# Slots' tables moved, a held weight piece loaded in the out-projection, router sums copied by two engines, the sample's last columns in one store

## The reference

```python
# u, bg, q, k, v, gates = _project(x, w_in, ...)   one input projection, two head groups
# conv_out = short gated convolution;  attn_out = attention with compressed, selected and window branches
def _post(x, conv_out, attn_out, p, w_out_l, norm_ffn_l, moe_w, norm_ple_l, w_ple_l, w_pg_l, b_pg_l):
    h = x + jnp.concatenate([conv_out, attn_out], axis=-1) @ w_out_l          # out-projection
    hn = rms_norm(h, norm_ffn_l)
    h = h + moe_ffn(hn.reshape(-1, D_MODEL), *moe_w).reshape(h.shape)         # experts
    gate = jax.nn.sigmoid((rms_norm(h, norm_ple_l) @ w_pg_l).astype(jnp.float32) + b_pg_l.astype(jnp.float32))
    return h + (gate * (p @ w_ple_l).astype(jnp.float32)).astype(h.dtype)     # gated embedding

def moe_ffn(h, w_rg, b_rg, w_re, b_re, w_g, w_u, w_d):      # cut: what is computed, not how it is blocked
    p_grp = jax.nn.softmax((h @ w_rg) + b_rg, axis=-1)      # 4 groups
    grp = jnp.argmax(p_grp, axis=-1)                        # the first of them
    le_g = the 8 logits of (h @ w_re) + b_re that belong to grp
    w2, e_loc = lax.top_k(jax.nn.softmax(le_g, axis=-1), 2) # two experts of 32
    w2 = w2 / jnp.sum(w2) * p_grp[grp]
    # for each chosen expert e:  y += w2 * ((silu(h @ w_g[e]) * (h @ w_u[e])) @ w_d[e])
```

## Time and profile before

| | |
|---|---|
| time, median of 3 runs | 905.92 us (903.79 to 905.94) |
| the profiled execution's own time | 907.63 us |
| its span in the trace | 905.7 us |
| PE busy | 888.5 us (98%) |
| DVE busy | 656.8 us (73%) |
| ACT busy | 204.3 us (23%) |
| POOL busy | 70.1 us (8%) |
| moved by DMA | 262.83 MB, mean 290 GB/s |

### The profile page before, as it was taken

The page is one execution under the profiler, slowest core; times in us unless marked ns, Lnnn a source line. Parts: engine busy times, 40 slices in busy tenths (PEclk is TensorE's granted clock), DMA queues, the critical chain, the costliest instruction groups (busy, mean ns, idle before and its releaser), DMA issues.

```text
span 905.7 us, 11854 instructions
## 1 busy us (share of the span) xinstructions
PE 888.5 (98%) x4539; PEld 464.1 (51%) x4539; DVE 656.8 (73%) x1290; ACT 204.3 (23%) x475; POOL 70.1 (8%) x72
## 2 busy tenths in 40 slices
PE   8999999999999999999999999999999999999998
PEld 7866998776544446444333433334434333333544
DVE  6568986668767764565867768678687686757895
ACT  4122231018645204411111111111111111111411
POOL 4021061000000000110000000000000000000000
PEclk9999999999999999999999999999999999999999
DMA  9752835530008776899999999999999999999502
GB/s 302 221 200 71 248 98 173 185 123 1 1 1 194 287 268 228 314 380 422 416 428 426 425 424 427 425 424 425 427 420 423 420 422 421 420 423 379 215 24 76
DMA packets 70269, 262.83 MB, mean 290 GB/s; under 512 B 11882, under 2 KB 38006, under 8 KB 53412
## 3 DMA queue, kind: packets, MB, share of 16 engines
q1 hardware_dynamic: 64864, 250.73, 70.9%
q0 software_dynamic: 4080, 8.93, 2.9%
q10 hardware_dynamic: 1268, 2.40, 0.7%
HBM read 254.95 MB, written 13.08 MB: 296 GB/s over the span
## 4 chain that ended last, share of the span: by engine, by line
PE 82%; DMA 9%; DVE 4%; SPq 3%; ACT 1%; issue 1%; POOLq 0%; DVEq 0%; ACTq 0%
PE ps L1451 75%; DMA w<-in_w_exp_down 4%; DMA w<-in_w_exp_up 4%; SPq L522 3%; PE ps L1946 2%; PE ps L2233 1%; PE ps L1475 1%; DMA h<-in_x_prompt 1%; PE ps L2274 1%; DMA xg<-hn_rows,sidx 1%; PE ps L1486 0%; PE ps L1949 0%; PE ps L1749 0%; PE ps L1639 0%; DVE probs L3098 0%
## 5 line engine op out<-in xcount | busy, mean ns | idle before, releaser
L1451 PE MATMUL ps<-w,xe 128*64 128x512 f32 x1024 | 228.1, 596 | 3.6 <-DMA w<-in_w_exp_up 3.5
L3516 DVE TENSOR_TENSOR h<-h,ps 128x1024 f32<-128x1024 f32 x120 | 143.2, 1215 | 104.6 <-PE ps L1451 104.5
L1451 PEld LDWEIGHTS ps<-w,xe 128*64 128x64 f32 x1024 | 70.1, 137 | 142.8 <-issue 134.1
L1451 PE MATMUL ps<-w,hT 128*64 128x512 f32 x504 | 115.4, 599 | 2.0 <-DMA w<-in_w_exp_down 2.0
L1451 PE MATMUL ps<-yk,ST 128*128 128x512 f32 (+1 forms) x320 | 105.2, 431 | 0.1
L1392 ACT ACTIVATE sg<-ps 64x256 f32<-64x256 f32 x64 | 24.1, 377 | 245.0 <-PE ps L1451 244.6
L984 POOL DMA_INDIRECT xg<-hn_rows,sidx x32 | 31.9, 998 | 611.7 <-PE ps L2233 375.3
L1451 PEld LDWEIGHTS ps<-yk,ST 128*128 128x128 f32 (+1 forms) x320 | 48.5, 174 | 56.3 <-issue 27.2
L1403 ACT ACTIVATE yk<-ps 64x512 fp32r<-64x512 f32 x64 | 38.0, 593 | 148.2 <-PE ps L1451 147.4
L1451 PEld LDWEIGHTS ps<-w,hT 128*64 128x64 f32 x504 | 33.3, 136 | 69.2 <-issue 69.0
L1451 PE MATMUL ps<-xT,wring 128*128 128x272 f32 x192 | 54.0, 408 | 0.0
(11 more groups left out here) (478 smaller groups left out, 1216.1 us busy)
## 6 DMA issues: line engine op xcount, KB each, us to landing
w<-in_w_exp_down SPq DMA_DIRECT2D x27, 2048.0 KB, 28.2
w<-in_w_exp_gate SPq DMA_DIRECT2D x32, 1024.0 KB, 30.3
w<-in_w_exp_up SPq DMA_DIRECT2D x32, 1024.0 KB, 31.1
w<-in_w_exp_gate SPq DMA_DIRECT2D x14, 2048.0 KB, 17.4
w<-in_w_exp_up SPq DMA_DIRECT2D x14, 2048.0 KB, 22.4
w<-in_w_exp_down SPq DMA_DIRECT2D x9, 1024.0 KB, 12.1
wring<-in_w_in SPq DMA_DIRECT2D x12, 512.0 KB, 6.8
h<-in_x_prompt SPq DMA_DIRECT2D x8, 512.0 KB, 6.0
```

The source lines that it names most:

```text
L1451: return nc.tensor.matmul(out, l, r, start=start, stop=stop, skip_group_check=skip)
L3516: TTn(h[0:r, t, :], h[0:r, t, :], both(b, r), ALU.add).then_inc(S["hadd"], 1)
```

## The change

Five edits, of which the first three belong together. `R` moves to where `hotS` was (72.25 K), and `hotS` to 76 K. Nothing of the router then lies at `free2`, so `early[0]` is loaded as soon as product 3 is done instead of after the slot sums. `hotS` now lies where `hnt[1]` does, so DVE waits for the five writes of `hn_rows` before it makes `hotS`. For the last tile ACT copies only the first set of router sums and DVE the second; `lg_ok` counts one more. Of the sample's last columns each half goes out in one transfer from SP, with the four quarters as the outermost dimension of the destination, and ACT issues none.

```diff
@@ tensors
-        hotS = at("hotS", [P, 2 * TT, SLOTS], 72.25 * K)
+        hotS = at("hotS", [P, 2 * TT, SLOTS], 76 * K)
+        R = at("R", [P, 2 * TT, 2, NE], 72.25 * K)
-        R = at("R", [P, 2 * TT, 2, NE], free2)
@@ the sample's stores
-        def sample_rows_out(eng, q, k):
-            eng.dma_start(o["y_sample"][:, q * 256 + k * P:q * 256 + (k + 1) * P], zs[NS * q:NS * (q + 1), k * P:(k + 1) * P])\
-                .then_inc(S["f_out0"], 16)
+        def sample_rows_out(eng, k):
+            y = o["y_sample"].rearrange("s (q n) -> q s n", q=4)[:, :, k * P:(k + 1) * P]
+            eng.dma_start(y, zs[:, k * P:(k + 1) * P]).then_inc(S["f_out0"], 16)
@@ SP
             sp.wait_ge(S["op_done"], product_done(3))
+            sp.dma_start(early[0][:], held[:, 0:1024]).then_inc(S[f"wc{CC - 1}"], 16)
             sp.wait_ge(S["op_h"], upto("w12", "w2", "w1"))
...
-            sp.wait_ge(S["lg_ok"], 2)
+            sp.wait_ge(S["lg_ok"], 3)
             load_piece(sp, 2, G0, 2)
...
             embed_out(5, 1, 0, D)
-            sp.wait_ge(S["sl_ps"], 1)
-            sp.dma_start(early[0][:], held[:, 0:1024]).then_inc(S[f"wc{CC - 1}"], 16)
             embed_out(6, 2, 0, D)
...
-                    for q in range(2):
-                        sample_rows_out(sp, q, k)
+                    sample_rows_out(sp, k)
...
-            sp.wait_ge(S["f_out0"], 16 * (2 * TP + 8))
+            sp.wait_ge(S["f_out0"], 16 * (2 * TP + 2))
@@ ACT
-                for p0 in (0, 64):
+                for p0 in (0,) if t == TP - 1 else (0, 64):
                     last = A(lgT[p0:p0 + NG + NE, turn(t) % 2, 0:r], ps[p0:p0 + NG + NE, 7, 0:r], C)
...
-            for k in range(2):
-                act.wait_ge(S["f_o"], block_no(("s", k)))
-                for q in range(2, 4):
-                    sample_rows_out(act, q, k)
@@ PE, the logits of the last tile
-                    pe.wait_ge(S["lg_ok"], 1)
+                    pe.wait_ge(S["lg_ok"], 2)
@@ DVE
             dve.sem_inc(S["lg_ok"], 1)
+            dve.wait_ge(S["r_done"], routed("products", TP - 1))
+            V.tensor_copy(lgT[64:64 + LW, turn(TP - 1) % 2, :], ps[64:64 + LW, 7, 0:P]).then_inc(S["lg_ok"], 1)
             dve.wait_ge(S["r_done"], routed("logits", TP - 1))
...
+            dve.wait_ge(S["hn_out"], 16 * TT)
             for k in range(2):
                 TTn(hotS[:, k * TT:(k + 1) * TT, :], along(C_IO, SLOTS)[:, 0:TT, :], sin[:, k, :].unsqueeze(2).broadcast_to([P, TT, SLOTS]),
```

## The result

The changed kernel takes 908.21 us, the median of 20 runs (905.08 to 910.29), against 905.36 us of the kernel before in 20 runs beside them: ratio 1.0032 [1.0024, 1.004], 2.9 us slower. The prediction had 906.3 us (+0.4 us) and "within 0.3%", in a range of 903.9 to 908.6 us. The measured time lies in that range, near its upper end, and the change is slower by just over the 0.3%; the interval of the ratio runs from 0.24% to 0.40%, so on which side of 0.3% it lies isn't settled. The profiled execution of the changed kernel has a span of 905.5 us and took 907.40 us itself, one of the shorter of the 20, so what lengthens the median is only in part in this trace. That is the first thing to notice, and the experiments are about it.

What follows compares the result with a forecast made beforehand. PE and a never-pausing weight stream bound the expert stage, both moving with PE's start on expert 0. Start +0.57 us and last store -0.2 us sum to +0.4 us: 906.3 us, range 903.9 to 908.6 us.

Steps and rivals of the forecast that it cites:

- The dearest case: Rival in the routing: the first gather still takes 5.32 us; +1.9 us in all, 907.8 us, chance 0.12.
- slower with a lower clock: Rival: rows land late or PE's new idle gap lowers its clock; slower by over 0.3%, chance 0.07.
- The wait: Ahead of hotS: DVE waits for the last hn_rows write, landing at 375.7 us; hotS starts 2.05 us later.
- The gather: First gather of routed rows: 3.4 us instead of 5.32 us, landing 0.5 us before PE is free.
- as slow as before: Rival: 5.32 us is the gather's own length, not the held piece's doing; +1.9 us in all, chance 0.12.
- The expert's start, +0.57 us: PE's start on expert 0: 0.57 us later, 1.48 us of former idling absorbing the rest; bounds +0.4 to +2.05 us.
- Router sums by two engines: Last tile's router sums: DVE copies beside ACT, 0.27 us gained up to the logits, swallowed by the new wait.
- The held piece in the out-projection at nothing: SP's queue at about 318 us: loading 0.52 MB early costs nothing; without cover, 1.2 us later landings.
- The last store, -0.2 us: End of kernel: single store issued at 903.15 us, landing 1.8 us later; -0.2 us, bounds -0.45 and +0.35.
- by pieces that is 1.76 us: Last store's landing time, interpolated by piece count between 1.6 us for 32 pieces and 2.4 us for 512.
- the last store is slow: Rival at the end: few engines carry the store, landing in 2.4 us; +0.35 instead of -0.2 us, chance 0.25.
- The clock: PE's 2.0 us gap near 374 us could lower its clock; countered by the expert stage's wait and clock 1.00.

Runs made afterwards that it cites:

- e3: Kernel before with only hotS and R moved, the held half piece loaded in the out-projection and DVE's wait for hn_rows added: 909.41 us, ratio 1.0021.
- f1: The changed kernel run again unaltered, as a yardstick on the second set's chip: 908.76 us, ratio 1.0024 to the kernel before.
- f2: Changed kernel with PE repeating half of tile 2's embedding projection ahead of the slot sums, DVE's wait kept: 908.10 us, ratio 1.0012 to the kernel before.
- f3: Changed kernel with the old eight stores of the sample's columns: 909.98 us, ratio 1.0028 to the kernel before.
- f4: Changed kernel with the old stores and hotS cut into two tables at free places, so without the hn_rows wait: 905.81 us, ratio 0.9988 to the kernel before.
- g4: Repeat on a third chip of the changed kernel with old stores, two hotS tables, no hn_rows wait and early held piece: 905.71 us, 0.999 to before.
- g2_swap: Changed kernel with old stores, second half of tile 2's projection moved ahead of the slot sums, wait kept: 906.84 us, ratio 1.0004 to the kernel before.
- e2: Kernel before with only the sample's last columns sent in one store per half: 908.83 us, ratio 1.0016.
- e4: Kernel before with only DVE's wait for the five hn_rows writes added ahead of hotS: 909.54 us, ratio 1.0024.
- e1: Kernel before with only the last tile's router sums copied by two engines: 907.27 us, ratio 0.9997.
- g3: Changed kernel with old stores, two hotS tables and no hn_rows wait, but held piece loaded after the slot sums: 906.70 us, 1.0000 to before.
- g1: Changed kernel with old stores, expert 2's 1 MB gate piece issued behind an embedding store, wait kept: 905.74 us, ratio 0.9989 to the kernel before.

## Why the prediction was partly right

That the time fell within the range owes something to luck. The dearest case that the range was built from was +1.9 us (907.8 us), and only the 0.8 us added for the runs' spread took in 908.21 us. The direction and most of the mechanism were right; the size, +0.4 us for 2.9 us, was not, and the case that came about, slower with a lower clock, had been given 0.07.

*The wait.* The mechanism held as written: hotS released by the last hn_rows write, PE idle some 2 us (2.38), the gather short, no idle time before the turn, one for one into the stream, no change in the expert stage. Landing was foreseen at 375.7 us; it came at 374.6 us in an execution whose routing lay 1.3 us earlier, so 0.2 us off by distance.

*The gather.* 3.4 us was taken, 2.8 us measured; hidden either way. The rival "as slow as before" didn't come about. The held piece was what drew it out: with the piece early, seven traces have 2.7 or 2.8 us (after, e3, f1 to f4, g4) and g2_swap 3.0 us; with it late, five have 4.0 to 5.8 us (e2 4.0, e4 4.2, e1 4.5, before 5.3, g3 5.8).

*The expert's start, +0.57 us.* The profiled pair gives +0.49 us. But the term rested on 1.48 us of PE idling for the gather in one execution. In the traces of e1_logits and e2_store, whose order here is that of before, the gather took 4.5 and 4.0 us, and gate and up start 20.82 and 20.44 us after ACT's copy instead of 21.76; after, f1_after and f2_fill have 22.25, 21.93 and 21.98. Three against three, the step is 22.05 - 21.01 = +1.0 us. The cover was overestimated by half a microsecond, and the range of the term, which ran to +2.05, held it. g3_nowait_late, with a gather of 5.8 us and 22.06 us, shows how far it scatters.

*Router sums by two engines.* Swallowed by the wait, as expected. The term was oversized: DVE's logits come 0.17 to 0.18 us sooner after ACT's copy (e1_logits, after), not 0.27 us, as DVE's copy takes 0.30 us itself. Alone it is within the measurement.

*The held piece in the out-projection at nothing.* Nothing in the traces contradicts it: SP issues it at 316.56 us, and the router sums of the last tile start no later with it than without (363.3 and 363.4 us on the average of nine and five traces).

*The last store, -0.2 us.* Wrong in sign: +0.4 us. From the last add to the end it takes 2.98 to 3.02 us in the four traces with the one store (after, e2_store, f1_after, f2_fill) and 2.54 to 2.64 us in the ten with the old ones. The estimate counted pieces and took no notice of how they are spread. The step that failed is "by pieces that is 1.76 us"; the rival "the last store is slow" (+0.35) is what happened. The Trainium skill's rule on the split of a copy ("DMA: Bandwidth & Descriptors", section "Why a DMA increments its semaphore by 16 and not by 1"), cited against the change beforehand, would give four engines, a share of 0.25; the 0.25 to 0.30 measured here agree nearly. SP's issue of it also took longer, 0.58 us for one, where two of the old ones took 0.78 us.

*The clock.* This is the step that failed most. The prediction named a lower clock and set it aside, because the longest wait of the expert stage is as long and the clock there reads 1.00. That reading doesn't carry it: the row ends at 830 us and PE's wait at 829.98 us, so it holds none of the work behind the wait, which is where the clock falls in other executions. In the profiled one it stayed at 1.00 behind it too (830 to 832 us), but that was one execution. Kernels in which PE idles for the write (after, f1, e3, e4, f3) have a mean clock below 0.9985 in 45 of 68 executions, the kernel before in 18 of 105; those in which the gap is filled or gone (f2, f4, g1 to g4) in 4 of 69. And behind the expert stage's own wait the clock does fall at times, as e3_tables shows at 834 us and g1_g0late at 829 us. In the changed kernel all executions together have a mean 1.8 us above the six at high clock (908.17 and 906.37 us), in f1_after 1.05 us; in the kernel before the same difference is 0.3 us (906.80 and 906.52 us beside f1_after). Weighted by their 20 and 12 runs the two give 1.5 us, less 0.3 us: the clock is worth about 1.2 us. This is an estimate; the 0.9 us between f1_after and f2_fill and the 1.7 to 3.1 us of a fall in the traces are in keeping with it. That the gap brings the falls is shown by f2_fill, which changes only what PE does in the gap.

In sum: +1.0 (start of the experts) + 0.4 (store) + 1.2 (clock) = +2.6 us, where +0.4 us was predicted and 2.9 us measured (2.2 us in f1_after). The first and the last term are means over few traces and scattered runs; that they add up so closely is partly chance.

Three things are open. Executions of e1_logits and e2_store had a low clock in 10 of 24, though PE has no new gap in them (before: 8 of 35 beside them). Their falls weren't caught in a profile; g1_g0late's was, behind the expert stage's wait, which all 14 traces have with 1.6 to 2.0 us, so theirs may lie there. PE's idle time alone doesn't decide it either: g3_nowait_late idles 1.97 us for the gather, ahead of the turn, and has a low clock in none of 12. And why the same gap lowers the clock in one execution and not in the next, no run tells: the profiled after had 2.38 us at a clock of 1.00, f3_oldstore 1.96 us and a fall.

## What to carry to other kernels

A wait put on the engine that feeds PE has two prices: the time that it moves the path, and the chance that PE's clock falls in the work behind the idle time; the second need not show in one profiled execution, so list the mean clock over many runs, and fill or close the gap. The slack that is to pay for a new wait scatters from run to run like the transfer it comes from; price it over several traces. Before moving a table onto another's place look at what store is still pending there and what is queued ahead of that store: moving one 1 MB load behind it was worth as much as finding a free place.

## What was not expected of the hardware

- After PE had been idle for 2.0 to 2.5 us its granted clock fell to 0.50 in some executions and not in others, each time in the work behind the gap, for some 3 us in e3_tables and over 5 us in f3_oldstore; a projection took 3.78 us for 1.98.
- A write of 0.5 MB took from 4.1 us (g1_g0late) to 9.67 us (g2_swap) to land, by when it was issued and what was queued with it; a gather of 0.26 MB 2.8 us (after) to 5.8 us (g3_nowait_late).
- A last store of 128 pieces of 512 bytes kept a steady 0.25 to 0.30 of the engines busy where the stores of 32 such pieces rose to 0.54 in bursts, and ended 0.43 us later.
